# One scattered tile of each expert stage gated on ScalarE and added on GpSimd; sums, norms and stores in another order and in halves

## What is computed

```
def rmsnorm(x, g):
    y = x * rsqrt(mean(x * x, axis=-1) + 1e-6)
    return y * g

# hier_moe: top-1 of 4 groups, top-2 of its 4 experts
top_w = softmax(top_v) * g_w
gates = sum(one_hot(eid, 16) * top_w[..., None], axis=1)
hid = silu(einsum('nd,edf->nef', xf, w_gate)) * einsum('nd,edf->nef', xf, w_up)
y = einsum('nef,efd->nd', hid * gates[..., None], w_down)

# per layer: x = x + mixer(rmsnorm(x)); x = x + hier_moe(rmsnorm(x)); at the end rmsnorm(x, norm_final)
```

## Time and profile before

| what | value |
|---|---|
| median of 3 executions | 586.61 us (585.15 to 587.17) |
| the profiled execution | 584.05 us, of which the span from first to last instruction is 581.9 us |
| TensorE busy (matmul) | 558.2 us, 96% of the span |
| VectorE, ScalarE, GpSimd busy | 247.4 us, 154.7 us, 79.4 us |
| mean granted TensorE clock | 0.995 of full speed |
| mean DMA rate | 359 GB/s |
| end of layer 0's expert stage | from about 252 to 275 us of the span |
| end of layer 1's expert stage | from about 561 to 581.9 us, the end of the span |

### The profile page before, as it was taken

The page is one execution under the profiler, slowest core; times in us unless marked ns, Lnnn a source line. Parts: engine busy times, 40 slices in busy tenths (PEclk is TensorE's granted clock), DMA queues, the critical chain, the costliest instruction groups (busy, mean ns, idle before and its releaser), DMA issues. The chain is left out here.

```text
span 581.9 us, 8509 instructions
## 1 busy us (share of the span) xinstructions
PE 558.2 (96%) x3438; PEld 309.4 (53%) x3438; DVE 247.4 (43%) x559; ACT 154.7 (27%) x327; POOL 79.4 (14%) x116
## 2 busy tenths in 40 slices
PE   6999999999999999998999999999999889999993
PEld 5777877544633333337876556667644533333331
DVE  6999783223651112145633415260113642211146
ACT  6132195121301101134235104164003220101023
POOL 5960800000121110000100001000000011220000
PEclk9999999999999999999999999999999999999997
DMA  8995999997999999999999998999699999999872
GB/s 329 415 355 79 222 401 380 375 403 318 363 410 420 419 419 422 395 306 374 390 412 317 409 400 335 304 355 409 256 407 417 381 406 417 420 419 423 358 234 91
DMA packets 40073, 208.94 MB, mean 359 GB/s; under 512 B 12835, under 2 KB 14563, under 8 KB 24192
## 3 DMA queue, kind: packets, MB, share of 16 engines
q1 hardware_dynamic: 30560, 169.93, 74.9%
q0 software_dynamic: 7872, 34.53, 16.6%
q10 hardware_dynamic: 1600, 3.90, 1.7%
HBM read 198.77 MB, written 43.74 MB: 417 GB/s over the span
## 5 line engine op out<-in xcount | busy, mean ns | idle before, releaser
L1513 PE MATMUL bank<-arena 128*64 128x512 f32 x264 | 85.6, 598 | 0.5 <-DVE arena L1853 0.5
L1513 PE MATMUL bank<-ring,arena 128*64 128x512 f32 x232 | 74.7, 598 | 0.1
L2310 PE MATMUL bank<-arena,ring 128*128 128x320 f32 x256 | 71.6, 434 | 0.0
L2310 PEld LDWEIGHTS bank<-arena,ring 128*128 128x128 f32 x256 | 48.0, 190 | 21.4 <-issue 1.6
L1434 PE MATMUL bank<-ring,arena 128*128 128x512 f32 x92 | 40.3, 594 | 1.0 <-PEq L455 0.6
L1513 PEld LDWEIGHTS bank<-arena 128*64 128x64 f32 x264 | 24.0, 136 | 31.5 <-issue 31.3
L1544 PE MATMUL bank<-arena 128*64 128x512 f32 x136 | 39.8, 594 | 0.7 <-ACT arena L1758 0.7
L577 PE MATMUL bank<-xnT,ring 128*128 128x320 f32 x144 | 39.5, 434 | 0.5 <-DVE xnT L896 0.5
L1969 DVE COPY arena<-bank 128x512 f32<-128x512 f32 x14 | 9.7, 692 | 68.3 <-PE bank L1544 68.3
L1544 PE MATMUL bank<-ring,arena 128*64 128x512 f32 x120 | 36.1, 593 | 0.7 <-ACT arena L1758 0.7
L1513 PEld LDWEIGHTS bank<-ring,arena 128*64 128x64 f32 x232 | 20.8, 136 | 24.5 <-issue 24.3
(11 more groups left out here) (446 smaller groups left out, 846.5 us busy)
## 6 DMA issues: line engine op xcount, KB each, us to landing
arena<-in_w_moe SPq DMA_DIRECT2D x50, 1024.0 KB, 17.4
ring<-in_w_moe SPq DMA_DIRECT2D x44, 1024.0 KB, 17.2
arena<-in_stream_b SPq DMA_DIRECT2D x4, 2560.0 KB, 14.8
out_o_d_old<-in_cache_d_g POOLq DMA_DIRECT2D x1, 8448.0 KB, 30.4
arena<-in_stream_a SPq DMA_DIRECT2D x4, 2048.0 KB, 10.8
out_o_d_old<-in_cache_d_g POOLq DMA_DIRECT2D x1, 7680.0 KB, 41.9
out_o_d_old<-in_cache_d_g SPq DMA_DIRECT2D x1, 4608.0 KB, 37.8
ring<-in_w_out_even SPq DMA_DIRECT2D x2, 2048.0 KB, 11.3
```

What stands on the lines that cost most here:

```text
L1513: last = nc.tensor.matmul(c.bank[2 + j % 2][half, :], xgT[:, j % 2, q, half], w[i][q // 4][:, q % 4, :], start=(q == 0), stop=(q == KC - 1))
L2310: last = nc.tensor.matmul(bank(name)[:, 0:TOK], w[:, k, i * P:(i + 1) * P], xnT[:, k, :], start=(k == 0), stop=(k == KC - 1))
```

## The change

In both layers one tile's scattered rows are taken from VectorE (tile 1, layer 1) or from TensorE (tile 2, layer 0): ScalarE multiplies them by their gates in place (`scale_rows`, 1024 columns, twice), and GpSimd adds them to the residual (two adds over 1024 columns). In layer 0 the diagonal matrices and their four matmuls go away, and tile 0's sums, norm and turn come ahead of tile 1's scattered rows. In layer 1 tile 2's last two multiplications go from VectorE to GpSimd (in two instructions), and tile 1's sums, squares, last multiplication and store are done in two halves of 512 columns.

```
-SUM_FIRST = (6, 5)
+SUM_FIRST = 5
+POOL_TILE = (2, 1)
...
             if layer == 0:
                 sp.wait_ge(earlier_ok, 2)
-                sp.wait_ge(sum_pe, sum_first + 6)
+                sp.wait_ge(gather_steps, 4)
+                sp.wait_ge(sum_pe, sum_first + 7)
                 c.load_item(sp, IT_Q)
...
                 for t in order:
                     rows_ready(sp, sems, t)
-                    sp.dma_start(out[t], next_rows[t][0:ROWS[t]]).then_inc(rows_final, 16)
+                    if sems is next_norm and t == 1:
+                        sp.dma_start(out[t][:, 0:512], next_rows[t][:, 0:512]).then_inc(rows_final, 16)
+                        sp.wait_ge(sems["rows1"], 2)
+                        sp.dma_start(out[t][:, 512:D], next_rows[t][:, 512:D]).then_inc(rows_final, 16)
+                    else:
+                        sp.dma_start(out[t], next_rows[t][0:ROWS[t]]).then_inc(rows_final, 16)
...
+            t = POOL_TILE[layer]
+            r = c.resid[0:ROWS[t], t]
+            for q in range(2):
+                pool.wait_ge(scaled, q + 1)
+                nc.gpsimd.tensor_tensor(r, m["yp"][t][0:ROWS[t], q * D:(q + 1) * D], r, ALU.add).then_inc(gather_steps, 1)
+                pool.wait_ge(gather_steps, 3 + q)
+            if layer == 1:
+                pool.wait_ge(next_norm["rstd"], 2)
+                pool.wait_ge(g_in, 16)
+                nc.gpsimd.tensor_scalar(next_rows[2][0:64], c.resid[0:64, 2], c.stat[0:64, 14:15], None, ALU.mult).then_inc(gather_steps, 1)
+                pool.wait_ge(gather_steps, 5)
+                nc.gpsimd.tensor_tensor(next_rows[2][0:64], next_rows[2][0:64], final_g[0:64], ALU.mult).then_inc(next_norm["rows2"], 1)
...
             sum_samples(0)
-            if layer == 0:
-                sum_rows(0, 1, 0)
             pe.wait_ge(yo_a, PAIR_N)
             sum_rows(1, 0, 0)
             pe.wait_ge(yo_b, PAIR_N)
             sum_rows(1, 0, 1)
-            if layer == 0:
-                sum_rows(0, 1, 1)
-                sum_rows(1, 1, 0)
-                sum_rows(1, 1, 1)
-                pe.wait_ge(yp_in[2], 16)
-                pe.wait_ge(diag_ok, 1)
-                for q in range(2):
-                    for h in range(2):
-                        nc.tensor.matmul(c.bank[0][64 * h:64 * h + 64, :], m["diag"][0:64, q, :],
-                                         m["yp"][2][0:64, q * D + h * 512:q * D + (h + 1) * 512], start=False, stop=False)
-            else:
+            if layer == 1:
                 sum_samples(1)
-                for h in range(2):
-                    sum_rows(0, 1, h)
-                    sum_rows(1, 1, h)
+            for h in range(2):
+                sum_rows(0, 1, h)
+                sum_rows(1, 1, h)
...
+            def scale_rows(t):
+
+                rows = ROWS[t]
+                for q in range(2):
+                    act.wait_ge(yp_hi if layer == 1 and q == 1 else yp_in[t], 16)
+                    part = m["yp"][t][0:rows, q * D:(q + 1) * D]
+                    nc.scalar.activation(part, part, ACT.Copy, scale=m["ok"][0:rows, q, t:t + 1]).then_inc(scaled, 1)
...
+                def square_halves(t):
+
+                    parts = c.stat[:, 0:1], c.stat[:, 9 + t:10 + t]
+                    for h in range(2):
+                        act.wait_ge(summed, 3 + h)
+                        half = slice(h * 512, h * 512 + 512)
+                        nc.scalar.activation(squares[t][:, half], c.resid[:, t, half], ACT.Square, accum_out=parts[h]).then_inc(sems["sq"], 1)
+                        if h == 0:
+                            act.wait_ge(sems["sq"], 3)
+                            nc.scalar.activation(c.stat[:, 1:2], parts[0], ACT.Identity, scale=1.0 / D, bias=c.eps).then_inc(sems["sq"], 1)
+                    act.wait_ge(sems["sq"], 5)
+                    nc.scalar.activation(parts[1], parts[1], ACT.Sqrt, scale=1.0 / D, bias=c.stat[:, 1:2]).then_inc(sems["rms"], 1)
...
                 scale(0)
+                if layer == 0 and sems is next_norm:
+                    scale_rows(POOL_TILE[0])
...
             nc.scalar.activation(c.stat[:, 15:16], c.stat[:, 15:16], ACT.Sqrt)
+            if layer == 1:
+                scale_rows(POOL_TILE[1])
...
             if layer == 0:
                 earlier_rows(0)
-                earlier_rows(1)
                 add_rows(sum_first, 0, 0)
                 add_rows(sum_first + 1, 0, 1)
-                next_mean(next_norm, 0)
-                add_rows(sum_first + 3, 1, 0)
-                add_rows(sum_first + 4, 1, 1)
+                earlier_rows(1, lambda: next_mean(next_norm, 0))
+                add_rows(sum_first + 4, 1, 0)
                 next_gain(next_norm, 0)
-                add_rows(sum_first + 5, 2, 0)
-                add_rows(sum_first + 6, 2, 1)
+                add_rows(sum_first + 5, 1, 1)
+                dve.wait_ge(gather_steps, 4)
+                add_rows(sum_first + 6, 2, 0)
+                add_rows(sum_first + 7, 2, 1)
...
                 earlier_rows(0)
-                earlier_rows(1)
...
                 next_rows_of(next_norm, 0, 0)
+                dve.wait_ge(gather_steps, 4)
                 add_rows(sum_first + 5, 1, 0)
+                next_mean(next_norm, 2)
                 add_rows(sum_first + 7, 1, 1)
-                next_mean(next_norm, 2)
-                next_rows_of(next_norm, 2, 0)
                 next_mean(next_norm, 1)
-                next_rows_of(next_norm, 1, 0)
+                final_halves(1)
```

More of the change, by code:

```diff
@@ L1193, in moe_block @@
     lg_read, lt_pe, lt_ok = s("logits_read"), s("pe_logitsT"), s("logitsT")
-    diag_ok = yp_hi = s(("diag", "rows_in1_hi")[layer])
+    yp_hi = s("rows_in1_hi") if layer == 1 else None
+    scaled = s("rows_scaled")
     summed, cnt_ok, g_in, rows_final = s("summed"), s("overflow_count"), s("final_gain"), s("final_out")
@@ L1203, in moe_block @@
     v_end = 3 * E_N + 1
-    final_g, next_rows = c.ring[:, 0:D], [m["xn"][:, i] for i in (0, 2, 1)]
+    final_g, next_rows = c.ring[:, 0:D], [m["xn"][:, 0], m["xn"][:, 2], m["xn"][:, 1] if layer == 0 else m["yp"][2][:, 0:D]]
     S_ok, first_out = s("onehot"), s("first_rows_out")
@@ L1221, in moe_block @@
     spare_base = [16 * layer * len(range(FIRST_PIECES + i, PIECES, PLACES[0])) if i < PLACES[0] - FIRST_PIECES else 0 for i in range(SPARE)]
-    n_parts, sum_first, order = len(parts), SUM_FIRST[layer], NEXT_ORDER[layer]
+    n_parts, sum_first, order = len(parts), SUM_FIRST, NEXT_ORDER[layer]
+    all_stored = 64
     ahead = ({(0, 0): 4, (0, 1): 4}, {(0, 1): OUT_AHEAD})[layer]
@@ L1374, in _ @@
                 if layer == 1:
-                    sp.wait_ge(rows_final, 48)
+                    sp.wait_ge(rows_final, all_stored)
                     for t, rows in enumerate(ROWS):
@@ L1382, in _ @@
                     store(norm_again)
-                    sp.wait_ge(rows_final, 96)
+                    sp.wait_ge(rows_final, all_stored + 48)
             if layer == 1:
-                sp.wait_ge(rows_final, 48)
+                sp.wait_ge(rows_final, all_stored)
                 sp.wait_ge(copies, n_copies)
@@ L1700, in _ @@
                     pe.wait_ge(w_in, 48)
-                    pe.wait_ge(summed, 3)
+                    pe.wait_ge(summed, 4)
                     for t, rows in enumerate(ROWS):
@@ L1790, in norm_steps_of @@
                 scale(0)
+                if layer == 0 and sems is next_norm:
+                    scale_rows(POOL_TILE[0])
                 square(order[1])
                 root(order[1])
-                square(order[2])
-                root(order[2])
+                if layer == 1 and sems is next_norm:
+                    square_halves(1)
+                else:
+                    square(order[2])
+                    root(order[2])
                 scale(2)
             nc.scalar.activation(c.stat[:, 15:16], c.stat[:, 15:16], ACT.Sqrt)
+            if layer == 1:
+                scale_rows(POOL_TILE[1])
             norm_steps_of(next_norm, [(summed, n + 1) for n in range(3)],
@@ L2001, in earlier_only @@
                 link(v.tensor_tensor(m["ok"], m["ok"], m["early"].unsqueeze(1).broadcast_to([P, 2, 3]), ALU.mult))
-                if layer == 0:
-                    for q in range(2):
-                        ins = v.tensor_tensor(m["diag"][0:64, q], c.ident[0:64, 0:64], m["ok"][0:64, q, 2:3].broadcast_to([64, 64]), ALU.mult)
-                    ins.then_inc(diag_ok, 1)
             def earlier_rows(t, between=None):
@@ L2011, in earlier_rows @@
                 for q in range(2):
-                    dve.wait_ge(yp_hi if layer == 1 and t == 1 and q == 1 else yp_in[t], 16)
+                    dve.wait_ge(yp_in[t], 16)
                     ins = v.scalar_tensor_tensor(r, m["yp"][t][0:rows, q * D:(q + 1) * D], m["ok"][0:rows, q, t:t + 1], r, ALU.mult, ALU.add)
@@ L2042, in add_rows @@
```

(13 more changed lines are left out.)

## The result

The changed kernel takes 593.0 us (median of 5 executions, 590.06 to 593.46), the kernel before 586.92 us (5 executions, 585.15 to 588.3). The ratio is 1.010, with a 95% interval of 1.007 to 1.013: slower by 6.1 us. The forecast was 589.4 us, 586.0 to 592.0. The direction was right, the size was not: the loss is more than twice the forecast one, and outside the range.

The account below looks back on a forecast made before the run. TensorE was taken to bound the kernel almost to the end, then ScalarE and VectorE alternating up to the last store. Layer 0's +0.25 and layer 1's +2.58 on 584.05, plus 2.56 to the median, gave 589.4 us, range 586.0 to 592.0.

Parts of the forecast that it names:

- GpSimd's one-input multiplication: Layer 1, first of GpSimd's two multiplications on tile 2: priced at 0.95 us from a memset row.
- T: Layer 1, start of tile 1's first sum on VectorE: 573.30 us before, forecast 1.65 us later.
- the anchor: TensorE's last row of sums in layer 1, 568.89 us before; the stretch up to it was forecast +0.25 us.
- x: Both layers, time of one GpSimd add over 1024 columns: taken as 2.3 us, likely 2.19 to 2.5.
- the rival of a slower add: Both layers: GpSimd's add takes 2.6 to 3.05 us, giving 590.9 to 593.1 us; chance 0.12.
- VectorE waits for GpSimd: Layer 1: VectorE's two-SBUF-input multiplications wait for a whole GpSimd instruction; tile 0's then takes some 3.3 us.
- The rival by which VectorE doesn't wait: Layer 1: tile 0 is multiplied at once, the total change is +1.15 us, 587.8 us; chance 0.16.
- The break-even at an add of 1.74 us: Whole sum, 5x - 8.7: the change neither gains nor loses when GpSimd's add takes 1.74 us.
- whom tile 2's products block: Layer 1: GpSimd's two-input product on tile 2 holds off VectorE's first half of tile 1 until T + 4.2.
- Layer 0: End of layer 0: earlier turn and start at 264.3, then a wait for tile 2's sums until 267.8; +0.25 us.
- the store's 0.3 us: End of layer 1: the last store, half as large, lands 0.3 us sooner after its issue.
- The clock rival: Layer 0: TensorE's two idle pieces drop the clock to 1.2 GHz, +3 to +10 us, 592.4 at least; chance 0.05.

Follow-up runs that it names:

- the price alone: Changed kernel plus eleven GpSimd instructions on dead tiles behind the last store, five of them beside eight VectorE products: 621.33 us, one execution, extra work included.
- the tail taken away: Changed kernel with tile 2's last multiplication in layer 1 back on VectorE as one instruction: 589.67 us, ratio 1.0047 to the kernel before.
- the order alone: Changed kernel with SyncE storing tile 1's halves ahead of tile 2: 589.36 us in one execution.
- the first experiment: Layer 0 as changed, layer 1 as in the kernel before: 587.06 us against 586.39, ratio 1.0005.
- the third: Changed kernel with dummy matmuls keeping TensorE busy in both idle pieces of layer 0: 591.63 us against 586.39 for the kernel before, ratio 1.0088.

## Why the prediction came out as it did

**The step that failed: "For GpSimd's one-input multiplication I take the 0.95 us of the memset of 64 x 1024".** It takes 2.85 us. A memset reads no tensor and computes nothing, and the trace of before held no better row; but this term was the only one of GpSimd's for which I set no upper end, though the add was bounded with care; its own upper slope, 3.05 us for 1024 columns, would have held the 2.85. With 2.85 in its place tile 2 is ready at T + 0.94 + 2.85 + 2.67 and the small gaps between, T + 6.54, instead of T + 4.23. That changes which tile is last. The prediction had tile 2's issue over at T + 4.75 and ahead of tile 1's; measured, tile 1 has been finished for 2.2 us when tile 2 arrives. Both tile 1's stores then go out behind it, 0.49 + 0.58 + 0.64 us for three issues in a row. The experiments show each part: the price alone (2.85), the tail taken away (-3.35), the order alone (-1.16).

The term is 1.90 us short, of 3.27 by which the span's loss was missed (6.10 against 2.83), and so the largest part but not all. With it the same sum would have said about 591.3. The rest is small pieces: 0.40 ahead of the change, 0.37 more up to the anchor, 0.27 more in the tail (the second product took 2.67 instead of 2.3, the issues came closer behind it), 0.44 behind the last issue, less the 0.11 by which T came sooner.

The Trainium skill says in "GPSIMD Engine Reference", section Engine selection, that GpSimd is about twice as slow as VectorE with two inputs and roughly at line rate with one. The first part agrees (2.34 us here against VectorE's 1.28). The second doesn't hold for the multiplication: 2.85 us is more than with two inputs. The copy, 1.03 us, comes nearest to it.

**Right: the add.** x = 2.3 was forecast; two of them took 4.77 and 4.78 us in the two layers, the gap between them counted, and one took 2.34 by itself. That also puts out the rival of a slower add: the 593.0 us lie inside its 590.9 to 593.1, but by luck, since it needed 2.6 us or more. **Right: VectorE waits for GpSimd.** Tile 0's multiplication took 3.31 us, about 3.3 forecast, and T moved by 1.54 us, 1.65 forecast. The rival by which VectorE doesn't wait is out: 3.25 us against 1.28 in the measurement of its own. The break-even at an add of 1.74 us was worked out with the 0.95 in it and doesn't stand either. A slip without effect: the 16-column row at 18.63 us is an addition, and not a product.

**Half right: whom tile 2's products block.** I had GpSimd's work on tile 2, by then its two-input product, hold off tile 1's halves until T + 4.2. The halves ran through in 1.42 us beside the first of the two, and it was GpSimd's second product that waited a little (2.67 us instead of 2.34). The Trainium skill, "SBUF — State Buffer", section "SBUF: two separate sides", gives the shared port for the whole instruction to whichever starts first, a VectorE instruction with two SBUF inputs or a GpSimd instruction that reads SBUF. The rows agree for the two-input instruction: VectorE loses 1.97 of its 2.34 us. For the one-input multiplication they don't: 2.85 us long alone, it costs VectorE 0.7.

**Layer 0: mechanism right, size off by half a microsecond.** +0.25 was forecast, +0.75 measured (and +0.74 with layer 0 alone). The turn, the start on the weights and the second idle piece all came. From the stage's last sums to the second `next_first` it took 14.01 us, forecast 13.63: GpSimd started 0.23 us later than the sum had it and its two adds took 0.12 more than the 4.65 reckoned. The remaining 0.1 us is an error of reading: the start of the second `next_first` before, 267.57, was taken as half of a row of 3.84 us. By the turn behind it, which comes 1.88 us after that start in the changed kernel, it was 267.44.

**Wrong, small: the store's 0.3 us.** The last store, of 256 KB, took 3.5 us from issue to landing. The 3.0 are the median of two of 512 KB; the last of them took 3.3. The issue to end distance didn't shorten, neither here nor with the halves alone.

**The clock rival is out as the cause of the loss,** by the windows, by the first experiment and by the third, although its 592.4 us at least covers the 593.0 measured. What it describes can happen: it did in one of six traces with this layer 0 and TensorE idle in it, and cost 1.64 us there, not the 3 to 10 forecast. It also did in one of three with layer 0 as before. The 3 us between the profiled execution and the median are a spread of whole executions that the kernel before shows as well. What makes the clock fall in some of them stays open.

Without GpSimd's tail the sum of layer 0 and of T is 0.75 + 1.54 = 2.3 us. The kernel with tile 2 back on VectorE is just that, and it is slower by 0.47% of 586.62 = 2.8 us, with 0.26% to 0.69% as its interval. That it is the same 2.8 as the forecast is chance: the forecast had +1.23 - 0.3 for the tail, which that kernel doesn't have, and less for layer 0.

## What to carry to other kernels

Price each operation of an engine by a row of the same operation; where there is none, bound it upward by the engine's dearest rate per column rather than taking a fill, and look at who queues behind its result in a fixed order, since a late tile holds the finished one behind it. A two-input instruction moved from VectorE to GpSimd, where it runs beside VectorE's own two-input products, isn't taken off VectorE: it comes back as a wait of up to its length (2.0 of 2.3 us here). Here it came back because the two met: with the product elsewhere in VectorE's order T came 1.1 us sooner. And separate the parts before judging them: a reordering worth some 0.9 us was covered by the move that came with it.

## What the runs showed of the hardware

- GpSimd's `tensor_scalar` multiplication of fp32: 2.85 us for 1024 columns and 1.56 for 512; `tensor_tensor` 2.34 and 1.26; `tensor_copy` 1.03. The multiplication takes 2.85 us for 64 partitions and for 128.
- Beside GpSimd's two-input instructions VectorE's two-input product takes 3.25 to 3.31 us instead of 1.28, and GpSimd's 3.19 instead of 2.34: they take turns. Beside the one-input multiplication VectorE loses only 0.66 to 0.74 us.
- SyncE's issue of a half tile's store takes 0.34 us when it stands alone, 0.58 and 0.64 right behind another issue (0.05 us apart).
- Between executions of one kernel the mean clock varied, in the kernel before from 0.987 to 0.996, and the span by up to 7 us (581.0 to 588.1). Where a trace shows the clock at half for about 3.4 us in layer 0, its stage is 1.64 us longer.
